# Eight neighbouring weight rows per partition, and half of the next gate weights split inside the SiLU

## The reference

```python
def expert_block(args):
    xb, e = args
    return (jax.nn.silu(xb @ w_gate[e]) * (xb @ w_up[e])) @ w_down[e]
```

## Time and profile before

| | |
|---|---|
| median of 3 runs | 1797.27 us (1796.37 to 1798.35) |
| the profiled execution | 1796.17 us, of which the span in the profile is 1794.4 us |
| PE (matmul) busy | 1625.1 us, 91% of the span |
| PEld (weight load) busy | 1411.8 us, 79% |
| DVE (VectorE) busy | 1271.1 us, 71% |
| ACT (ScalarE) busy | 931.0 us, 52% |
| POOL (GpSimd) busy | 309.9 us, 17% |
| DMA queue of SP | 312.37 MB in 170524 packets |

### The profile page before, as it was taken

How to read it: one execution, slowest core, us unless ns; L and a number is a source line. 1 busy time by engine, 2 the same in 40 slices (tenths; PEclk the granted TensorE clock), 3 DMA queues, 4 the chain that set the end, 5 groups by cost and what they waited for, 6 DMA issues and landing times. The chain is left out here.

```text
span 1794.4 us, 26138 instructions
## 1 busy us (share of the span) xinstructions
PE 1625.1 (91%) x10760; PEld 1411.8 (79%) x10760; DVE 1271.1 (71%) x1509; ACT 931.0 (52%) x1138; POOL 309.9 (17%) x187
## 2 busy tenths in 40 slices
PE   3679999999989999999798997499999999999956
PEld 2459988998889999998797785388888888888842
DVE  2535276637767678685766447789999999999947
ACT  2624233623544536363202121578888888888843
POOL 0110000200110201011200000133533232323230
PEclk9789999999999999999899998699999999999988
DMA  9822101310120202114254435699999999999976
GB/s 349 322 50 60 50 24 37 106 33 25 37 90 25 89 25 69 45 41 167 84 182 151 150 112 184 226 346 374 374 381 378 381 374 373 365 380 371 379 259 246
DMA packets 186563, 345.98 MB, mean 193 GB/s; under 512 B 16034, under 2 KB 71946, under 8 KB 185356
## 3 DMA queue, kind: packets, MB, share of 16 engines
q1 hardware_dynamic: 170524, 312.37, 49.0%
q0 software_dynamic: 9824, 17.88, 2.7%
q10 hardware_dynamic: 6096, 14.04, 2.1%
HBM read 316.15 MB, written 43.83 MB: 201 GB/s over the span
## 5 line engine op out<-in xcount | busy, mean ns | idle before, releaser
L140 PE MATMUL x_psum_proj<-h_hi,x_w_hi 128*128 128x364 f32 (+1 forms) x1120 | 380.9, 340 | 9.5 <-ACT x_x L796 6.2
L141 PE MATMUL x_psum_proj<-h_lo,x_w_hi 128*128 128x364 f32 (+1 forms) x1120 | 369.8, 330 | 0.0
L142 PE MATMUL x_psum_proj<-h_hi,x_w_lo 128*128 128x364 f32 (+1 forms) x1120 | 369.6, 330 | 0.0
L140 PEld LDWEIGHTS x_psum_proj<-h_hi,x_w_hi 128*128 128x128 f32 x1120 | 211.9, 189 | 17.9 <-ACT x_x L796 7.4
L141 PEld LDWEIGHTS x_psum_proj<-h_lo,x_w_hi 128*128 128x128 f32 x1120 | 212.1, 189 | 2.4
L142 PEld LDWEIGHTS x_psum_proj<-h_hi,x_w_lo 128*128 128x128 f32 x1120 | 212.0, 189 | 0.0
L572 POOL CAST x_w_hi<-x_w 128x1024 fp32r<-128x1024 f32 x44 | 73.6, 1674 | 636.5 <-PE x_psum_proj L142 634.1
L1978 POOL DMA_INDIRECT scratch_y<-e_y,all_tbl x32 | 87.4, 2732 | 369.8 <-ACT e_y L2089 357.2
L1186 DVE TENSOR_REDUCE x_sc<-x_diag 64x64 f32<-64x448 f32 x136 | 126.7, 931 | 1.1
L140 PE MATMUL e_psum_g<-e_g_hi,e_x_hi 128*128 128x512 f32 x256 | 105.1, 410 | 16.8 <-DVE e_x_lo L2213 16.6
L1211 DVE TENSOR_TENSOR x_w_lo<-x_w,x_w_hi 128x1024 fp32r<-128x1024 f32 x52 | 64.3, 1236 | 72.3 <-POOL x_w_hi L572 72.2
(11 more groups left out here) (350 smaller groups left out, 3757.6 us busy)
## 6 DMA issues: line engine op xcount, KB each, us to landing
mg_ring_hi<-in_w_e_gate SPq DMA_DIRECT2D x34, 1024.0 KB, 12.5
mg_ring_lo<-in_w_e_down SPq DMA_DIRECT2D x34, 1024.0 KB
mg_ring_hi<-in_w_e_up SPq DMA_DIRECT2D x32, 1024.0 KB, 10.3
mg_ring_lo<-in_w_e_up SPq DMA_DIRECT2D x32, 1024.0 KB
mg_ring_lo<-in_w_e_gate SPq DMA_DIRECT2D x30, 1024.0 KB
mg_ring_hi<-in_w_e_down SPq DMA_DIRECT2D x30, 1024.0 KB, 12.6
c_w<-in_w_ada SPq DMA_DIRECT2D x12, 2048.0 KB, 13.8
x_w<-in_w_in SPq DMA_DIRECT2D x44, 512.0 KB
```

Source lines behind the costliest of these rows:

```text
L140: nc.tensor.matmul(out, lhs[0], rhs[0], start=start, stop=False)
L141: nc.tensor.matmul(out, lhs[0], rhs[1], start=False, stop=False)
L142: return nc.tensor.matmul(out, lhs[1], rhs[0], start=False, stop=stop)
```

## The change

1. `weight_view` lays the rows so that partition p holds 8 neighbouring rows of a gate or up matrix (4 of a down matrix), where it held rows 128 apart. A half is then 4 rows of 2 KB (or 2 rows of 4 KB) next to each other in HBM for each partition.
2. So that the token side has the same order, the transposes take every eighth column of `xg` (x) and every fourth of `hid`.
3. The high part of the first half of gate(e+1) moves on ScalarE from behind the SiLU's last Exp to ahead of it, and its low part on VectorE from behind the third SiLU step to behind the first.

```diff
 def weight_view(a, part, e, half):
     name = {"g": "w_e_gate", "u": "w_e_up", "d": "w_e_down"}[part]
-    return a[name][0][e].rearrange("(k p) f -> p k f", p=P)[:, half_rows(part, half), :]
+    return a[name][0][e].rearrange("(p k) f -> p k f", p=P)[:, half_rows(part, half), :]
...
 # ScalarE
-            def high(part, e):
-                for half in range(2):
+            def high(part, e, halves=(0, 1)):
+                for half in halves:
...
                 nc.scalar.activation(hid[:, :], hid[:, :], ACT.Ln, bias=1.0).then_inc(silu_act, 1)
+                if e + 1 < NE:
+                    high("g", e + 1, (0,))
                 reach(act, silu_dve, 2 * e + 1)
                 nc.scalar.activation(hid[:, :], hid[:, :], ACT.Exp).then_inc(silu_act, 1)
...
-                    high("g", e + 1)
+                    high("g", e + 1, (1,))
...
 # VectorE
-            def low(part, e):
-                for half in range(2):
+            def low(part, e, halves=(0, 1)):
+                for half in halves:
...
                                        op0=ALU.min, op1=ALU.subtract).then_inc(silu_dve, 1)
+                if e + 1 < NE:
+                    low("g", e + 1, (0,))
                 reach(dve, silu_act, 4 * e + 4)
...
-                    low("g", e + 1)
+                    low("g", e + 1, (1,))
...
 # TensorE
+                cols = xg[:, e % 2, :].rearrange("n (p k) -> n k p", k=KD)
                 for k in range(KD):
-                    m = nc.tensor.transpose(p_x[:, k, :], xg[:, e % 2, k * P:(k + 1) * P], ident[0:N, 0:N])
+                    m = nc.tensor.transpose(p_x[:, k, :], cols[:, k, :], ident[0:N, 0:N])
...
+                cols = hid[:, :].rearrange("n (p f) -> n f p", f=KF)
                 for f in range(KF):
-                    m = nc.tensor.transpose(p_h[:, f, :], hid[:, f * P:(f + 1) * P], ident[0:N, 0:N])
+                    m = nc.tensor.transpose(p_h[:, f, :], cols[:, f, :], ident[0:N, 0:N])
```

## The result

| kernel | median us | runs, lowest to highest | profiled execution us (span) |
|---|---|---|---|
| before | 1796.82 | 4, 1794.84 to 1798.35 | 1796.17 (1794.4) |
| after | 1786.01 | 4, 1783.79 to 1786.87 | 1785.40 (1783.6) |

The ratio is 0.9938, 95% interval 0.9926 to 0.995. The change made the kernel 10.8 us faster, by the medians and by the two profiled executions alike. The forecast was 1817 us, slower; rival A had said 1784.

A forecast was written before the change was run, and what follows sets the result against it. The prediction took VectorE's order of work as the bound, TensorE 0.41 us behind. Period 18.13 - 0.41 + 1.14 = 18.86: 29 x 0.73 = +21.2, -1.7 and +0.3 give +19.8, so 1817 us; 8-in-10 range 1781 to 1824.

The forecast's parts named there:

- rival A: TensorE's transposes: a strided load stays under 0.11 us, so the kernel gains 13.6 us, to 1784; chance 0.30.
- The early half: Gate split moved ahead of the Exp: VectorE gains 1.1 us of idle, the period falls 0.41 us to 17.72.
- The matmul row's 0.18: TensorE's idle at the gate product by its matmul row: lower end of the period's gain, against 0.41 taken.
- The start of the stage: First two experts, where VectorE also waited for TensorE: `x_lo` about 0.85 us earlier twice, 1.7 us in all.
- A strided load is 128 x 1.75 = 0.224 us: TensorE's transposes of `x` and `hid`: 0.224 instead of 0.11 us, ten exposed loads, 1.14 us more per expert.
- A faster load is worth nothing: DMA side of the layout: no wait for a weight load, so longer runs were taken as 0 us.
- 5 us to spare: Down weights land 12.8 us after issue and are read by ScalarE 17.9 us after it.
- way of being wrong altogether: Named sign of failure: ScalarE begins to wait for a load, or the matmuls of 512 columns slow.
- B: TensorE's strided load takes twice its packed 0.069, so 0.138 us: period 18.00, kernel 1792; chance 0.10.
- C: TensorE's transposes: only the 32-byte step pays and `hid` is free: period 18.52, kernel 1807; chance 0.05.
- D: Changed order frees nothing, the Exp queuing behind a late split; loads stay hidden, period 18.13, kernel 1797; chance 0.05.
- The point where the cost eats the gain: Exposed strided load on TensorE at which the gain is gone: 0.11 + 0.44/10 = 0.154 us.

The follow-up runs named there:

- order_only: The changed kernel with its early half of the gate weights, but the old weight layout and packed transposes: 1795.61 us, ratio 0.9986 to the kernel before.
- gate_up_layout: The changed kernel with the old layout for the down weights (4 KB runs) and packed transposes of `hid`: 1785.78 us, ratio 0.9935 to the kernel before.
- pairs: The changed kernel with two neighbouring rows per partition for gate and up (4 KB runs), down as before, `hid` packed, `xg` stepping 8 bytes: 1787.13 us, ratio 0.9939 to before.

## Why the prediction was wrong

**The early half: right.** The order of ScalarE and VectorE came out as worked out, and the period without strided loads and without DMA waits is 17.713 us for the 17.72 forecast. The matmul row's 0.18 was rightly not taken.

**The start of the stage: about half.** `x_lo` of expert 3 (counted from 0) is 2.1 us earlier (1198.42 to 1196.34), but its gate product starts only 0.9 us earlier (1199.69 to 1198.81): the other 1.2 is VectorE running ahead of TensorE. So TensorE got 0.9 us for the 1.7 forecast. 0.9 + 10.5 = 11.4 is the lead at the last expert's down weights (1727.49 to 1716.09); at the end 10.8 are left.

**"A strided load is 128 x 1.75 = 0.224 us": the step that failed.** This is the term that was mis-sized. That a transpose takes as long as its load, once the load is longer than the stream, was right. But the load takes 0.111 us at 32 bytes and 0.117 to 0.120 at 16, against the 0.11 that the stream takes anyway. What strided loads cost is 17.760 - 17.713 = 0.05 us an expert, not 1.14. The sum had 29 x 1.14 + 0.3 = 33.4 us for them, and 28 x 0.047 = 1.3 came; these 32.1 us, less the 1.5 that the other terms fell short of their 13.6, are the 30.6 from the forecast's +19.8 to the measured -10.8. The error was to take VectorE's rate over strides for TensorE's. The agreement that decided for it, with TensorE's stream of four neighbours in 1.77 ns, is its rate of streaming columns, which no stride has a part in. The rows closest to the operation, left 0.04 us of room beside a packed load of 0.069 and had the better claim.

**"A faster load is worth nothing": wrong too, without moving the number.** The prediction added the order's full gain and 0 for the DMA. With the DMA of before, that gain doesn't exist: order_only got 1 us of it. Two readings misled me. "5 us to spare" was one stretch of a landing time that rose from 7.6 to 16.2 us through the stage. And the 400 to 430 GB/s of the earlier trace rows came from another stream, without gathers beside it. The rate of the earlier trace rows, 379 GB/s, is one period of a stage whose four stretches of 100 us from 1250 on moved 375, 380, 370 and 374: what the 2 and 4 KB runs gave, not a demand with room above. I had named this way of being wrong altogether (ScalarE waiting for a load) for the changed kernel, where the layout prevents it.

**The rivals.** A (load under 0.11, 1784) was nearly right: 0.376 us a period for its 0.41, and the missing 2.8 us are some 1.4 that come nearly all from the strided loads, which lie just above 0.11 instead of under it, 0.8 at the start and some 0.6 behind the last expert. B (0.138, the packed load doubled) has the mechanism: 0.120 is close to twice the 0.063 of a packed step, and 0.111 a little less; what it had too high is the figure that it doubled. C has it the wrong way round: the 16-byte step is dearer than the 32-byte one. D is refuted: the order frees what it should. The point where the cost eats the gain is a slip in the prediction: 13.6/29 = 0.47 us a period gives 0.157 us, not 0.154; nothing hangs on it.

**Still open.** Why runs of 2 and 4 KB give about 372 GB/s here. Short runs alone don't: the stream of the earlier trace rows moved 21.69 MB in 10227 packets, 2.1 KB each, from 0 to 60 us, most of it at 400 to 430 GB/s, and order_only moved 34.10 MB in 14474, 2.4 KB each, at 370. The gathers and scatters stand beside the second only; no run left them out. The number of packets (14474 against 4890 on the weights' queue in 100 us) goes with it in part only: gate_up_layout has fewer packets than pairs (8070 against 10906 in all) and its landing time rises nearly as fast. What rate 8 KB runs could reach wasn't measured; the changed kernel asks for 385 to 390.

## What to carry to other kernels

Read the issue-to-landing time of a steady stream at the start, the middle and the end of its stage: if it rises, the stream is already the bound and the lead is being spent, so an order that shortens the period must come with faster loads. Cost an operand's stride by rows of the same engine and port, and set it against the stream beside it, for only the longer of the two is paid; a rate from another engine is not a bound. Two edits that are worth nothing each can be worth their sum and more together, so try them together before dropping either.

## What the hardware did that I had not expected

- Transposes paced by TensorE's load of a float32 stationary tile with 128 columns: 0.063 us start to start packed (0.070 with the group's longer first step), 0.117 to 0.120 with steps of 8 and 16 bytes, 0.111 with 32. The price doesn't grow with the step.
- It is the same with 64 rows and 64 streamed columns as with 128 and 128: 0.119 in pairs (8 bytes), 0.111 in after (32 bytes). That is why pairs, with the shorter step, has the longer loads and period: mean load from 1250 to 1650 us 207 against 191 ns, periods 17.807 and 17.760. Why 32 bytes are cheaper than 8 and 16 stays open.

```profile
L2313 PEld LDWEIGHTS e_psum_x<-all_ident,e_xg 128*128 128x128 f32 x176 | 24.6, 207 | 1.7
```

- The same 1 MB loads with gathers beside them: 369 to 375 GB/s in runs of 2 and 4 KB with loads waited for; 382 to 390 GB/s and a landing time that still rises in runs of 4 KB, or 8 and 4; 385 to 390 GB/s and no rise from early to late only with 8 KB throughout.
